# A mixture-of-experts encoder layer on one core: the row gather gets a bound, and empty slots point beyond the table

## The chip, the core and the metric

The kernel runs on one core of a Trainium2 chip. The metric is device time in microseconds (us) for one execution. The time before is the median of 3 runs, 2170.36 us (2167.73 to 2170.91). A profiled execution of the same kernel took 2169.55 us, of which 2167.7 us lie between its first and last instruction (the span).

## The reference: what is computed

One layer over 512 tokens of width 2048, in float32. Four token mixers and an output product come first. What matters here is the second half, a mixture of experts: every token picks one of 4 groups and then 2 of that group's 8 experts, so 1024 assignments fall on 32 experts, and every expert is a gated MLP (2048 to 768 to 2048).

```python
lg = h32 @ w_group + b_group
grp = jnp.argmax(lg, axis=-1)
le = take_along_axis((h32 @ w_router + b_router).reshape(t, 4, 8), grp[:, None, None], axis=1)[:, 0]
top_p, top_i = lax.top_k(softmax(le), 2)
gate = p_grp * top_p / sum(top_p)
expert = grp[:, None] * 8 + top_i
...
a = silu(xblk @ w_gate[e]) * (xblk @ w_up[e])
y = a @ w_down[e]          # each row times its gate, summed per token
```

With the inputs of setup_inputs, the reference's routing gives the experts 0 to 31 these numbers of rows: 25 18, 17 12, 15 27, 26 30, 47 36, 21 52, 33 25, 34 30, 40 20, 47 32, 38 45, 34 44, 31 25, 27 32, 44 61, 26 30 (a comma after each pair of experts). Their sum is 1024, and the largest is 61.

## The kernel before, in words

The first 676 us hold the mixers, the output product, the second norm and the router logits. The normed rows are written to a table in HBM, `h2_dram` (512 rows of 8 KB), by SyncE (line 347). VectorE then works out for every assignment a slot number: expert times 64 plus the assignment's rank within the expert (lines 1122 to 1187). An expert has 64 slots; had one more than 64 rows, a second loop (lines 453 to 457 on GpSimd) would take what is over.

The experts are worked in 16 pairs. Pair i has 128 slots: rows 0 to 63 of a tile are the even expert's, rows 64 to 127 the odd one's, each filled from rank 0 upward. The plan of a pair is a product on TensorE (`plan`, line 827): a 0/1 matrix of slot against assignment (`pick`) times the two columns of `asg`, token number and gate. A slot that nobody has gets a sum of zero in both. VectorE reads the plan (`read_plan`): `planned` gets token numbers and gates, and `gidx` the token numbers as integers (line 1209). `make_back` compares `planned` with the row `tokens`, which puts each result row back to its token. The combine adds gate times row, so that an empty slot adds zero.

GpSimd gathers the pair's rows (`gather`, line 445): 128 rows of 8 KB from `h2_dram` into `hg` (which lies in region_h), one row for each partition, by `gidx`. The first gather waits for the first plan. Every later one waits until TensorE has transposed the rows of the pair before (`hte_ps`), and is needed one pair later.

TensorE transposes 64 rows at a time (`transpose_rows`, line 837), then takes for each expert four tiles of gate and up weights (line 859) and two of down weights (line 878), and between them combines the pair before (line 850). SyncE loads the 192 weight tiles of 3 MB each into a ring of 5 buffers (lines 331 and 333). Tiles 0 to 4 are issued before the experts start; tile n waits until TensorE has used tile n - 5 (`tile_used`). The ring's buffers and the gather's rows come through the same 16 DMA engines.

The names in the rows: region_rest, region_w and region_h are parts of SBUF that hold the ring; region_h also holds `hg`; banks is PSUM; h_rows is `h2_dram`.

Of the kernel before, what the change touches and what calls it, by code (L numbers as in the profile page):

```python
# [26 lines left out]
ALU = mybir.AluOpType  # L27
# [3 lines left out]
P = 128  # L31
T = 512
# [4 lines left out]
NT = T // P  # L37
# [16 lines left out]
OVER = 2 * T // SLOTS  # L54
NA = 2 * NT
BIG = 1e30
UK = 4
NU = KT // UK
UNITS = NCH * NU
# [13 lines left out]
def build(nc, x, mix_norm, w_in, w_fourier, w_spatial, b_spatial, conv_w, w_pool, pool_scale, out_norm,  # L73
# [3 lines left out]
    with ctx:  # L77
        def sem(name):
            return ctx.enter_context(nc.semaphore(name))
# [10 lines left out]
        ps = ctx.enter_context(nc.psum_tensor("banks", [P, 8, 512], F32))  # L90
        h2_dram = nc.dram_tensor("h2_rows", (T, D), F32).ap()

        def at(off, *dims):
            n = int(np.prod(dims))
            r = min(off // R, 4)
            off -= r * R
            v = regions[r][:, off:off + n]
            if len(dims) == 2:
                v = v.rearrange("p (a b) -> p a b", a=dims[0])
            if len(dims) == 3:  # L100
                v = v.rearrange("p (a b c) -> p a b c", a=dims[0], b=dims[1])
            if len(dims) == 4:
                v = v.rearrange("p (a b c d) -> p a b c d", a=dims[0], b=dims[1], c=dims[2])
            return v
# [7 lines left out]
        h_lo = split_w1[:, 0:KT * T].rearrange("p (a b) -> p a b", a=KT)  # L112
        w_raw = [at(W0 + s * 8 * KB, UK, DG) for s in range(NU)]
        w_hi, w_lo = ([split_x[:, o:o + UK * DG].rearrange("p (a b) -> p a b", a=UK) for o in (c, c + 16 * KB)]
                      for c in (0, 8 * KB))
# [37 lines left out]
        tokens = at(o, T)  # L153
# [12 lines left out]
        asg = at(o, NT, 2, 2); o += NA * 2  # L166
        slot = at(o, NT, 2); o += NA
        gidx = [at(o + k, 1).bitcast(U32) for k in (0, 1)]; o += 2
# [12 lines left out]
        hg = at(H + 24 * KB, D)  # L181
# [80 lines left out]
        xo_ps, x2_stored = sem("xo_ps"), sem("x2_stored")  # L262
# [6 lines left out]
        counted, over_ready = sem("counted"), sem("over_ready")  # L269
        pick_ready, plan_ps, plan_read = sem("pick_ready"), sem("plan_ps"), sem("plan_read")  # L270
        slots_shifted = sem("slots_shifted")
        rows_gathered = sem("rows_gathered")
        hte_ps, hte_ready = sem("hte_ps"), sem("hte_ready")
        silu_ready, act_ready = sem("silu_ready"), sem("act_ready")
        at_ps, at_ready = sem("at_ps"), sem("at_ready")
        tokens_ready = sem("tokens_ready")
# [8 lines left out]
        OUT_TILES = NT * 4  # L285
# [6 lines left out]
        def _(sp):  # L292
# [3 lines left out]
            def w_in_unit(chunk, q):  # L296
                sp.dma_start(w_raw[q], win_v[:, q * UK:(q + 1) * UK, chunk]).then_inc(w_landed[q], 16)

# [80 lines left out]
        @block.gpsimd  # L379
        def _(pool):  # L380
            n = 0

            def made(ins):
                nonlocal n
                n += 1
                ins.then_inc(consts, 1)
                pool.wait_ge(consts, n)

            g = nc.gpsimd
            made(g.memset(ident, 0.0))  # L390
            made(g.affine_select(out=ident, in_=ident, compare_op=ALU.not_equal, fill=1.0, base=0,
                                 pattern=[[-1, P]], channel_multiplier=1))
            made(g.memset(mean_w, 1.0 / DG))
            made(g.memset(eps, EPS))
            made(g.memset(ones, 1.0))

            made(g.affine_select(out=before, in_=ones, compare_op=ALU.is_gt, fill=0.0, base=0,
                                 pattern=[[1, P]], channel_multiplier=-1))
            made(g.iota(iota, [[1, P]], 0, 0, allow_small_or_imprecise_dtypes=True))
            made(g.iota(pri4, [[-1, G]], G, 0, allow_small_or_imprecise_dtypes=True))  # L400
            made(g.iota(pri8, [[-1, EG]], EG, 0, allow_small_or_imprecise_dtypes=True))
            made(g.iota(e64, [[SLOTS, E]], 0, 0, allow_small_or_imprecise_dtypes=True))
            made(g.iota(thr, [[SLOTS, NSPLIT]], SLOTS, 0, allow_small_or_imprecise_dtypes=True))
            made(g.iota(nums, [[1, OVER]], 0, 0, allow_small_or_imprecise_dtypes=True))
            made(g.iota(asg[:, :, :, 0], [[P, NT], [0, 2]], 0, 1, allow_small_or_imprecise_dtypes=True))

            for t in range(NT):
                for q in (1, 3):
                    pool.wait_ge(ht_hi, 4 * t + q + 1)
                    full, hi, lo = (h[:, 4 * q:4 * q + 4, t * P:(t + 1) * P] for h in (h_full, h_hi, h_lo))  # L410
                    g.tensor_tensor(lo, full, hi.bitcast(F32), ALU.subtract)\
                        .then_inc(ht_lo_pool, 1)


            def split_low(u, s, q):

                pool.wait_ge(w_hi_ready, u + 1)
                pool.sem_inc(turns, 1)
                g.tensor_tensor(w_lo[s], w_raw[q], w_hi[s].bitcast(F32), ALU.subtract).then_inc(w_ready, 1)  # L419

            pool.wait_ge(x_sq, NT)
            pool.wait_ge(ht_ps, 4 * NT)
            pool.wait_ge(w_ready, 1)
            split_low(1, 1, 1)
            split_low(2, 0, 2)
            split_low(3, 1, 3)
            with pool.Fori(1, NCH) as i:
                for q in range(NU):
                    split_low(i * NU + q, q % 2, q)

            for n in range(3):
                pool.wait_ge(sq_ready, 4 * n + 4)
                for m in range(1, NH):
                    g.tensor_tensor(sq[:, 0, :], sq[:, 0, :], sq[:, m, :], ALU.add).then_inc(sq_summed, 1)
                    pool.wait_ge(sq_summed, 3 * n + m)

            pool.wait_ge(logits_ps, NT)
            g.iota(tokens, [[1, T]], 0, 0, allow_small_or_imprecise_dtypes=True).then_inc(tokens_ready, 1)

            def gather(i, first=False):  # L440
                pool.wait_ge(plan_read, i * 5 + 5)
                if not first:
                    pool.wait_ge(hte_ps, i * 2)
                pool.sem_inc(turns, 1)
                g.indirect_dma_start(out=hg, out_offset=None, in_=h2_dram,  # L445
                                     in_offset=bass.IndirectOffsetOnAxis(ap=gidx[0], axis=0))\
                    .then_inc(rows_gathered, 16)

            for b in (0, 1):
                pool.wait_ge(h2_saved[b], 32)  # L450
            for i in range(PAIRS):
                gather(i, first=(i == 0))
            n_over = pool.value_load(over_i[0:1, OVER:OVER + 1], min_val=0, max_val=OVER)
            with pool.If(n_over > 0):
                with pool.Fori(PAIRS, PAIRS + OVER_PAIRS) as i:
                    gather(i)
                pool.wait_ge(rows_gathered, 16 * (PAIRS + OVER_PAIRS))
            pool.wait_ge(rows_gathered, 16 * PAIRS)
# [3 lines left out]
        def _(ae):  # L462
# [17 lines left out]
            def gains(landed, q):  # L480
                ae.wait_ge(w_landed[q], landed)
                for k in range(UK):
                    c = C_MIX + UK * q + k
                    a.activation(w_raw[q][:, k, :], w_raw[q][:, k, :], ACT.Copy, scale=cols[:, c:c + 1])\  # L484
# [453 lines left out]
        def _(ve):  # L938
            v = nc.vector
            done = 0  # L940

            def then(ins):

                nonlocal done
                done += 1
                ins.then_inc(dve_done, 1)
                ve.wait_ge(dve_done, done)
# [191 lines left out]
            for k in (0, 1):  # L1139
# [6 lines left out]
                if k == 0:  # L1146
                    then(v.scalar_tensor_tensor(les2, oh[:, 0], -BIG, les, ALU.mult, ALU.add))
                    cur = les2
# [53 lines left out]
            def read_plan(i, s):  # L1202
                ve.wait_ge(plan_ps, i + 1)
                low, high = slice(0, SLOTS), slice(SLOTS, 2 * SLOTS)
                v.tensor_copy(planned[low, s, 0::2], ps[low, 5, 0:2]).then_inc(plan_read, 1)
                v.tensor_copy(planned[high, s, 0::3], ps[high, 5, 0:2]).then_inc(plan_read, 1)
                v.tensor_copy(planned[low, s, 1::2], ps[high, 5, 0:2]).then_inc(plan_read, 1)
                v.tensor_copy(planned[high, s, 1:3], ps[low, 5, 0:2]).then_inc(plan_read, 1)
                v.tensor_copy(gidx[0], ps[:, 5, 0:1]).then_inc(plan_read, 1)

            def make_back(i, s):
                ve.wait_ge(tokens_ready, 1)
# [28 lines left out]

            compare()
            read_plan(0, 0)
            next_compare(1)

# [88 lines left out]
```

## Time and profile before

| what | value |
|---|---|
| median of 3 runs | 2170.36 us |
| profiled execution | 2169.55 us |
| its span | 2167.7 us |
| TensorE busy | 1942.9 us (90%) |
| VectorE busy | 499.8 us (23%) |
| ScalarE busy | 257.0 us (12%) |
| GpSimd busy | 165.6 us (8%) |
| moved by DMA | 691.19 MB |
| of that on the gather's queue, q0 | 16.78 MB in 2304 packets |

Busy time is the time in which an engine had an instruction under way. The share of the DMA is the mean over its 16 engines. "Landing" is the time from the issue of a transfer until its last byte is there. Waits are put down to the instruction or the transfer that came last.

### The profile page before, as it was taken

Reading aid. Unit: us, or ns where it says so; the run is one execution under the profiler, and the core shown is the slowest. Engines: PE = TensorE matmul, PEld = TensorE weight load, DVE = VectorE, ACT = ScalarE, POOL = GpSimd, SP = SyncE. Lnnn points to the kernel's source line nnn. Section 1 sums busy time; section 2 is a strip of 40 time slices with the busy share of each in tenths; the row PEclk is TensorE's granted clock in tenths of the full one; section 3 lists DMA queues with packets and bytes.
Section 4 is the critical chain, followed back from the end, with each engine's and each line's share of the span. In section 5 each row is a group of like instructions: output and inputs, shape, how many; then the busy total and the mean of one; then the engine's idle time right before and its main releaser. Section 6 shows DMA issues by size and latency. Waiting matters only on the chain.

```text
span 2167.7 us, 20657 instructions
## 1 busy us (share of the span) xinstructions
PE 1942.9 (90%) x9337; PEld 1018.8 (47%) x9337; DVE 499.8 (23%) x667; ACT 257.0 (12%) x369; POOL 165.6 (8%) x78
## 2 busy tenths in 40 slices
PE   6999999899995998889888898988988889988895
PEld 5887885344455443434434344343443334433342
DVE  4112115500034021122211221112212122221224
ACT  5222201300000010010000100001000010000102
POOL 4444440200000000000000000000000000000000
PEclk8999999999995899999999999999999999999998
DMA  6222213091015899999999999999999999999993
GB/s 255 97 96 87 89 39 113 0 354 72 20 58 233 343 430 429 431 428 430 429 430 429 429 429 429 430 430 429 430 429 430 430 428 431 429 429 431 428 430 160
DMA packets 63043, 691.19 MB, mean 319 GB/s; under 512 B 8769, under 2 KB 9969, under 8 KB 34034
## 3 DMA queue, kind: packets, MB, share of 16 engines
q1 hardware_dynamic: 55058, 670.64, 73.7%
q0 software_dynamic: 2304, 16.78, 1.9%
q10 hardware_dynamic: 5600, 2.54, 0.4%
q8 instruction: 69, 1.13, 0.2%
q14 instruction: 12, 0.10, 0.0%
HBM read 681.55 MB, written 8.39 MB: 318 GB/s over the span
## 4 chain that ended last, share of the span: by engine, by line
PE 49%; DMA 46%; DVE 3%; issue 1%; ACT 1%; ACTq 0%; POOL 0%; POOLq 0%; PEldq 0%; DVEq 0%
DMA region_rest<-in_w_gate 25%; PE banks L859 17%; PE banks L664 14%; PE banks L774 10%; DMA region_h<-in_w_gate 9%; DMA region_w<-in_w_gate 9%; PE banks L850 3%; DMA region_rest<-in_w_up 2%; DMA region_rest<-in_w_down 1%; PE banks L719 1%; PE banks L794 1%; PE banks L878 1%; DVE region_rest L1072 1%; PE banks L785 1%; DVE region_x L1293 0%
## 5 line engine op out<-in xcount | busy, mean ns | idle before, releaser
L859 PE MATMUL banks<-region_rest,region_w 128*64 128x384 f32 x2432 | 429.6, 508 | 70.8 <-DMA region_rest<-in_w_gate 55.9
L859 PEld LDWEIGHTS banks<-region_rest,region_w 128*64 128x64 f32 x2432 | 183.3, 142 | 309.2 <-issue 233.5
L1222 DVE TENSOR_TENSOR region_x<-banks,region_x 128x1024 f32<-128x1024 f32 x128 | 151.1, 1220 | 648.9 <-PE banks L850 648.8
L664 PE MATMUL banks<-split_h,split_x 128*128 128x512 f32 x896 | 279.8, 392 | 13.6 <-DVE split_x L995 10.3
L878 PE MATMUL banks<-region_rest,region_w 128*64 128x512 f32 x960 | 229.7, 633 | 25.9 <-DVE region_w L1240 13.0
L774 PE MATMUL banks<-region_w,region_h 128*128 128x512 f32 x512 | 220.8, 593 | 2.6 <-DVE region_h L1075 2.6
L664 PEld LDWEIGHTS banks<-split_h,split_x 128*128 128x128 f32 x896 | 169.4, 189 | 51.6 <-issue 16.4
L664 PE MATMUL banks<-split_w,split_x 128*128 128x512 f32 x448 | 175.3, 391 | 0.0
L859 PE MATMUL banks<-region_w 128*64 128x384 f32 x832 | 141.2, 493 | 19.8 <-DMA region_w<-in_w_gate 16.1
L859 PE MATMUL banks<-region_h,region_w 128*64 128x384 f32 x832 | 143.1, 498 | 15.0 <-DMA region_h<-in_w_gate 12.6
L774 PEld LDWEIGHTS banks<-region_w,region_h 128*128 128x128 f32 x512 | 97.0, 190 | 124.8 <-issue 118.9
L878 PEld LDWEIGHTS banks<-region_rest,region_w 128*64 128x64 f32 x960 | 69.7, 145 | 172.1 <-issue 132.4
L850 PE MATMUL banks<-split_w 128*128 128x512 f32 x512 | 138.2, 412 | 3.9 <-DVE split_w L1228 3.6
L419 POOL TENSOR_TENSOR split_x<-region_w,split_x 128x2048 fp32r<-128x2048 f32 x27 | 124.4, 4609 | 175.1 <-DVE split_x L955 175.1
L1228 DVE TENSOR_TENSOR split_w<-banks,split_w 64x1024 fp32r<-64x1024 f32 x64 | 78.1, 1220 | 233.8 <-ACT split_w L586 232.8
L850 PEld LDWEIGHTS banks<-split_w 128*128 128x128 f32 x512 | 92.8, 192 | 60.1 <-issue 35.9
L445 POOL DMA_INDIRECT region_h<-h_rows,region_rest x16 | 15.4, 962 | 1298.0 <-PE banks L837 1279.1
L859 PEld LDWEIGHTS banks<-region_w 128*64 128x64 f32 x832 | 60.4, 138 | 97.9 <-issue 74.5
L859 PEld LDWEIGHTS banks<-region_h,region_w 128*64 128x64 f32 x832 | 61.1, 139 | 93.8 <-issue 75.4
L484 ACT ACTIVATE region_w<-region_w,region_rest 128x512 f32<-128x512 f32 x112 | 71.6, 716 | 196.2 <-DMA region_w<-in_w_in 196.2
L591 ACT ACTIVATE region_w<-banks 128x384 f32<-128x384 f32 x32 | 15.7, 492 | 651.6 <-PE banks L859 651.6
L664 PEld LDWEIGHTS banks<-split_w,split_x 128*128 128x128 f32 x448 | 84.7, 189 | 17.6 <-issue 0.2
(185 smaller groups left out, 1032.9 us busy)
## 6 DMA issues: line engine op xcount, KB each, us to landing
region_rest<-in_w_down SPq DMA_DIRECT2D x40, 3072.0 KB, 31.0
region_rest<-in_w_gate SPq DMA_DIRECT2D x39, 3072.0 KB, 31.1
region_rest<-in_w_up SPq DMA_DIRECT2D x37, 3072.0 KB, 30.7
region_w<-in_w_up SPq DMA_DIRECT2D x14, 3072.0 KB, 31.0
region_h<-in_w_up SPq DMA_DIRECT2D x13, 3072.0 KB, 30.8
region_h<-in_w_gate SPq DMA_DIRECT2D x13, 3072.0 KB, 31.0
region_w<-in_w_gate SPq DMA_DIRECT2D x12, 3072.0 KB, 32.2
region_h<-in_w_down SPq DMA_DIRECT2D x12, 3072.0 KB, 31.1
```

The source lines that it names most:

```text
L419: g.tensor_tensor(w_lo[s], w_raw[q], w_hi[s].bitcast(F32), ALU.subtract).then_inc(w_ready, 1)
L484: a.activation(w_raw[q][:, k, :], w_raw[q][:, k, :], ACT.Copy, scale=cols[:, c:c + 1])\
L664: mm = t_.matmul(ps[:, bank + m, :], w[s][:, kk, cols_m], h[:, k, :], start=(k == 0 and w is w_hi and h is h_hi), stop=(k == KT - 1 and w ...
L719: mm = t_.matmul(ps[:, (h + 1) % 4, :], ab[:, s, h, c * HD:(c + 1) * HD], dft[:, c, s, :], start=(c == 0 and s == 0), stop=(c == 1 and s = ...
L774: mm = t_.matmul(ps[:, j % 3, :], yT[:, k, t * P:(t + 1) * P], wbuf[n % 2][:, k, :], start=(m == 0), stop=(m == KT - 1))
L785: mm = t_.transpose(ps[:, 4 + q, k * P:(k + 1) * P], h2[t % 2][:, c:c + P], ident)
L794: mm = t_.matmul(ps[:, 3, t * 64:t * 64 + G + E], h2T[:, k, :], wr[:, k, :], start=(k == 0), stop=(k == KT - 1))
L850: mm = t_.matmul(ps[:, 2 + 2 * c + n, :], back[c][:, t * P:(t + 1) * P], y[c][:, n * 512:(n + 1) * 512], start=(y is y_hi), stop=(y is y_lo))
L859: mm = t_.matmul(ps[h * SLOTS:(h + 1) * SLOTS, u, 0:HF], hTe[:, k, :], ring_gu[slot][:, kk, h * HF:(h + 1) * HF], start=(k == 0), stop=(k ...
L878: mm = t_.matmul(ps[g * SLOTS:(g + 1) * SLOTS, 6 + n, :], aT[:, kk, q * SLOTS:(q + 1) * SLOTS], ring_down[slot][:, kk, (2 * c + n) * 512:( ...
L1222: v.tensor_tensor(tile, ps[:, 2 + 2 * c:4 + 2 * c, :], tile, ALU.add).then_inc(comb_added, 1)
L1228: v.tensor_tensor(y_rows(y_lo, b, c), ps[g * SLOTS:(g + 1) * SLOTS, 6:8, :], y_rows(y_hi, b, c).bitcast(F32), ALU.subtract).then_inc(y_lo_ ...
```

## The change

Token numbers are kept with 4096 taken off, in `asg` and in `tokens`, by the start values of two iotas. The plan's sum for an occupied slot is then its token minus 4096, and for an empty slot still 0. `read_plan` adds 4096 as it writes `gidx`, so that an occupied slot has its token there and an empty one 4096. The gather is given a bound of 511 with no error beyond it: it passes over those slots, and the rows of `hg` there keep what they hold. So that this is a number from the start, GpSimd clears `hg` once, ahead of the first gather. The clearing waits for the last output product (`xo_ps`), whose operand lies in the same bytes, and the gathers behind it wait for the clearing.

```diff
+NOBODY = 4096
...
-            made(g.iota(asg[:, :, :, 0], [[P, NT], [0, 2]], 0, 1, allow_small_or_imprecise_dtypes=True))
+            made(g.iota(asg[:, :, :, 0], [[P, NT], [0, 2]], -NOBODY, 1, allow_small_or_imprecise_dtypes=True))
...
             pool.wait_ge(logits_ps, NT)
-            g.iota(tokens, [[1, T]], 0, 0, allow_small_or_imprecise_dtypes=True).then_inc(tokens_ready, 1)
+            g.iota(tokens, [[1, T]], -NOBODY, 0, allow_small_or_imprecise_dtypes=True).then_inc(tokens_ready, 1)
...
                 g.indirect_dma_start(out=hg, out_offset=None, in_=h2_dram,
-                                     in_offset=bass.IndirectOffsetOnAxis(ap=gidx[0], axis=0))\
+                                     in_offset=bass.IndirectOffsetOnAxis(ap=gidx[0], axis=0),
+                                     bounds_check=T - 1, oob_is_err=False)\
                     .then_inc(rows_gathered, 16)
 
+            pool.wait_ge(xo_ps, OUT_TILES)
+            g.memset(hg, 0.0).then_inc(rows_cleared, 1)
+            pool.wait_ge(rows_cleared, 1)
             for b in (0, 1):
                 pool.wait_ge(h2_saved[b], 32)
...
-                v.tensor_copy(gidx[0], ps[:, 5, 0:1]).then_inc(plan_read, 1)
+                v.tensor_scalar(gidx[0], ps[:, 5, 0:1], float(NOBODY), None, ALU.add).then_inc(plan_read, 1)
```

On GpSimd, ahead of the experts, the order before is: the iota of `tokens`, then the 16 gathers, then the code that looks whether a second loop is needed.

```order
L434 TENSOR_TENSOR region_w<-region_w 128x512 x9
L438 IOTA region_rest 128x512
L445 DMA region_h<-h_rows,region_rest 128x2048 x16
L453 TENSOR_LOAD region_rest
L453 ISA x2
```

At the same place of the changed kernel:

```order
L435 TENSOR_TENSOR region_w<-region_w 128x512 x9
L439 IOTA region_rest 128x512
L452 MEMSET region_h 128x2048
L446 DMA region_h<-h_rows,region_rest 128x2048 x16
L458 TENSOR_LOAD region_rest
L458 ISA x2
```

One instruction is new, the clearing of `hg` (128 partitions by 2048 elements), between the iota and the first gather. Nothing else is moved on GpSimd.

On VectorE, where the first plan is read (four copies to `planned`, then `gidx`), the order before is:

```order
L1191 TENSOR_TENSOR region_w<-region_rest 128x1024
L1205 COPY region_rest<-banks 64x2
L1206 COPY region_rest<-banks 64x2
L1207 COPY region_rest<-banks 64x2
L1208 COPY region_rest<-banks 64x2
L1209 CAST region_rest<-banks 128x1
L1198 TENSOR_SCALAR region_rest<-region_rest 128x8
```

And in the changed kernel:

```order
L1196 TENSOR_TENSOR region_w<-region_rest 128x1024
L1210 COPY region_rest<-banks 64x2
L1211 COPY region_rest<-banks 64x2
L1212 COPY region_rest<-banks 64x2
L1213 COPY region_rest<-banks 64x2
L1214 TENSOR_SCALAR region_rest<-banks 128x1
L1203 TENSOR_SCALAR region_rest<-region_rest 128x8
```

The cast of 128x1 has become an addition of 128x1 at the same place. The order is otherwise the same, here and on the other engines.

## Rows read from the trace of the kernel before

**Rows 1.** The page: DMA share in tenths and GB/s, in 40 slices

```profile
DMA  6222213091015899999999999999999999999993
GB/s 255 97 96 87 89 39 113 0 354 72 20 58 233 343 430 429 431 428 430 429 430 429 429 429 429 430 430 429 430 429 430 430 428 431 429 429 431 428 430 160
```

**Rows 2.** Four stretches: busy us (x instructions) of each engine, granted clock, DMA share, GB/s

```profile
698.00:705.00 7.00, 1.94 (x16) 1.78 (x16) 0.34 (x3) 0.28 (x1) 0.00 (x0) 0.50 0.84 300
705.00:714.00 9.00, 8.20 (x34) 3.31 (x36) 0.00 (x0) 2.03 (x2) 0.00 (x0) 0.63 0.01 2
714.14:2130.23 1416.09, 1268.03 (x6888) 573.08 (x6884) 297.35 (x381) 110.53 (x125) 14.07 (x15) 0.96 1.00 427
2130.23:2167.70 37.47, 16.89 (x56) 9.03 (x56) 22.03 (x18) 12.18 (x15) 0.00 (x0) 0.75 0.28 113
```

**Rows 3.** TensorE's waits from 714 to 2131 us: us in total, times, longest us

```profile
PE banks L859 <- DMA region_rest<-in_w_gate: 55.9, 27, 4.2
...
PE banks L859 <- DMA region_w<-in_w_gate: 16.1, 8, 2.6
PE banks L859 <- DMA region_rest<-in_w_up: 13.7, 9, 1.8
```

**Rows 4.** The page: DMA queues with packets, MB, share of 16 engines' span

```profile
q1 hardware_dynamic: 55058, 670.64, 73.7%
q0 software_dynamic: 2304, 16.78, 1.9%
```

**Rows 5.** The gathers of line 445: ns min/median/max, first and last start; then landing times

```profile
L445 POOL DMA_INDIRECT region_h<-h_rows,region_rest x16: 937/939/1319, 696.1 to 1989.7; - x16
  PE banks L837: 1279.1, 15
who waited for it (us, times):
  PE banks L837: 8.6, 1
...
DMA to landing us min/median/max: 6.5/14.4/15.8
```

**Rows 6.** The chain that ended last, around the first gather: start us, us, what

```profile
694.99 0.17 DVE region_rest L1209
...
696.14 6.52 DMA region_h<-h_rows,region_rest
...
702.75 1.95 PE banks L837 x16
...
704.72 1.03 ACT region_w L580
...
705.80 23.77 PE banks L859 x128
```

**Rows 7.** GpSimd's instructions at its start: start us, us, instruction

```profile
0.79 0.20 POOL L390 MEMSET region_rest<- 128x128 f32 x1 [0.29 <-POOLq L1324]
...
1.84 0.10 POOL L394 MEMSET region_rest<- 128x1 f32 x1
...
28.77 4.58 POOL L419 TENSOR_TENSOR split_x<-region_w,split_x 128x2048 fp32r<-128x2048 f32 x1 [3.57 <-DVE split_x L955]
```

**Rows 8.** GpSimd's instructions ahead of the first gather

```profile
676.70 0.56 POOL L438 IOTA region_rest<- 128x512 f32 x1 [264.69 <-PE banks L794]
696.14 1.32 POOL L445 DMA_INDIRECT region_h<-h_rows,region_rest  x1 [18.88 <-DVE region_rest L1209]
```

**Rows 9.** VectorE around the first plan

```profile
676.55 0.17 DVE L1125 TENSOR_REDUCE region_w<-region_w 128x4 f32<-128x16 f32 x1
...
694.99 0.16 DVE L1209 CAST region_rest<-banks 128x1 uint32<-128x1 f32 x1
695.06 0.16 DVE L1198 TENSOR_SCALAR region_rest<-region_rest 128x8 f32<-128x8 f32 x1
```

More of the change, by code:

```diff
@@ L271, in build @@
         slots_shifted = sem("slots_shifted")
-        rows_gathered = sem("rows_gathered")
+        rows_gathered, rows_cleared = sem("rows_gathered"), sem("rows_cleared")
         hte_ps, hte_ready = sem("hte_ps"), sem("hte_ready")
```

## The prediction

> **What bounds the kernel now.** I read the busy slices of the page first, to find the stage in which the changed code runs. From slice 15 on the DMA engines are busy for nine tenths or more of every slice but the last, at 428 to 431 GB/s, the weight stream of the experts [rows 1]. The table by stretch makes it sharper: from 714.14 us, when SyncE issues the first tile that had to wait for a free buffer, to 2130.23 us, when the product on the last tile starts, the DMA share is 1.00 at 427 GB/s, and TensorE is busy for 1268.03 of 1416.09 us [rows 2]. So TensorE has 148 us to spare there and the DMA engines have nothing.
>
> Next I asked what TensorE waits for in that stretch. Nine rows name weight tiles and sum to 125.5 us; the three longest are shown, in short waits of 4.2 us at most [rows 3]. That is a kernel that takes each tile soon after it has landed. The count of bytes agrees: 187 tiles of 3.146 MB and 15 gathers of 1.049 MB are 604 MB, and 604 MB at 427 GB/s is 1415 us. What leaves the 16 DMA engines in this stretch leaves the time, as long as TensorE keeps up. It has to make up at most about 20 us out of 148.
>
> **What the gathers cost now.** The gather's queue carries 16.78 MB, which is 16 times 128 rows of 8 KB, in 2304 packets; its share of the 16 engines' span is 1.9%, or 41 us [rows 4]. The price of one row: 427 GB/s over 16 engines is 26.7 GB/s for one engine, so 8192 bytes take it 0.307 us. Checked the other way, 128 rows to an engine in the whole run by 0.307 us are 39.3 us, near the 41. The latency of a gather costs nothing in the stretch: it lands 14.4 us after its issue in the median, and it is issued a pair (some 90 us) before it is needed. Only one wait on a gather is on record, 8.6 us, the first [rows 5].
>
> **The change part by part.**
>
> *Rows that are no longer moved.* The experts' counts (in the section on the reference) sum to 1024 of 2048 slots, so half of the slots are empty. Pair 0 has 43 rows, and pairs 1 to 15, whose gathers lie in the saturated stretch, have 981 of 1920; 939 rows go. If the bound makes the gather drop them, the mean DMA engine loses 939 / 16 = 58.7 rows, or 18.0 us. But a weight tile is usable only when all 16 engines have brought their part, so the time follows the engine that keeps the most gathered rows, not the mean. Slots fill from rank 0 upward, so the empty ones are always the high ranks of each half, and how rows are dealt to the engines decides. The trace of before can't show the deal, because with 128 rows each engine has 8 in any deal. The bounds are:
> - the live rows dealt evenly: 18.0 us off;
> - row number modulo 16: the engine with rank 0 keeps 73 of its 120 rows in pairs 1 to 15, 47 go, 14.4 us;
> - runs of four, an engine having ranks 4k to 4k+3 and the four ranks 32 higher of one half: the engine with ranks 0 to 3 and 32 to 35 of the even experts keeps four rows in each of the 15 pairs (60), all four more where the even expert has 36 rows or more (47, 40, 47, 38, 44: 20), and 1, 2 and 2 for the ones with 33, 34 and 34. That is 85 of 120; 35 go, 10.7 us;
> - runs of eight: the engine with ranks 0 to 7 keeps all 120, since every expert has more than eight rows, and nothing is gained.
>
> I take 10.7 us, the runs of four. It is the deal near the middle of 0 to 18.0. The page "DMA: Bandwidth & Descriptors" of the Trainium skill, section "The descriptor swizzle", gives for a plain transfer to 128 partitions just this deal: engine 0 writes partitions 0 to 3 and 32 to 35, engine 8 partitions 64 to 67 and 96 to 99. No run here has shown that a gather with dropped rows keeps to it; by that page the sum stays as it is, by an even deal it would be 7 us better.
>
> *The first gather.* It is in the open: issued at 696.14, it holds TensorE for 6.52 us, and behind it come in one chain the transposes, the copy on ScalarE, and the first expert's products, whose end frees the first ring buffer at 714.14 [rows 6]. The DMA engines are idle from 705 to 714 (share 0.01) [rows 2], so what the first gather saves starts the whole stream earlier. Pair 0 has 25 and 18 rows, and with them no engine has more than 4 rows in place of 8: 4 by 0.307 us is 1.2 us off. The bounds are 0 (the wait is latency alone) and 2.5 us (all 8 rows). I take 1.2. The skill's same page, section "Anatomy of one DMA", fits such a transfer as 2.0 us and its bytes at 436 GB/s; by that the first gather would lose 1.6 us, as an estimate, and the 2.0 us would stay.
>
> *The clearing.* Not in the trace at this size. On GpSimd a MEMSET of 128x1 takes 0.10 us and one of 128x128 0.20 us; in proportion 128x2048 is 0.10 + 16 times 0.10 = 1.7 us, and the two-operand TENSOR_TENSOR of 128x2048, 4.58 us, bounds it from above [rows 7]. It can start when the iota of 676.70 is done, at 677.3 (it follows the last router logits, which come after the last output product that the clearing waits for), and the first gather waits until 696.14 for another reason, the plan [rows 8]. So it is over by 682 at the latest, with 14 us to spare: 0 us. Behind it in GpSimd's queue is only that gather. With the cover gone it would cost 1.7 us once. It runs beside VectorE's routing chain, which is on the path; were VectorE held for all of it, that would cost 1.7 us, 4.6 at the most. I take 0, since no wait joins them.
>
> *The shifted numbers.* The two iotas only start from another value. The addition for `gidx` in place of the cast is one VectorE instruction for one: CAST 128x1 0.16 us, TENSOR_SCALAR 128x8 0.16 us [rows 9]. 0 us; were it slower, 15 of the 16 lie 90 us ahead of their use.
>
> *The bound itself.* The instruction of the gather takes GpSimd 0.94 us in the median [rows 5], and the comparison with 511 may lengthen it. Only the first would show. Below, 0; above, see the last rival. I take 0.
>
> **The sum.** 10.7 + 1.2 = 11.9 us off. The profiled execution, 2169.55 us, becomes 2157.6; from the median 2170.36, 0.8 us higher, it is 2158.5 us. Its own range, with the first gather at 0 to 2.5 us and up to 1.7 for VectorE beside the clearing, is 2157 to 2161.5.
>
> **The rivals.** What a measurement of this kernel can tell from no change is about 0.2%, or 4.3 us.
> - *The rows are spread more evenly* (modulo 16, or live rows alone dealt out). Then 14.4 to 18.0 us and 1.2 go: 2151 to 2155 us. For it: a gather walks a list and could deal out what is left. Against it: the destinations are fixed rows, as before. 0.30.
> - *The bound doesn't spare the slow engine.* Either an empty slot still costs its transfer (a row read and thrown away), or the deal is in runs of eight. Then the stream is as long as before, and at most the first gather is quicker: 2169 to 2170.4 us. For it: the trace has no gather with a bound. Against it: a row that lands nowhere need not be moved. 0.14.
> - *The check makes the gather slow to issue.* If GpSimd goes through the 128 indices one by one, at the price of a smallest instruction (0.10 us for a MEMSET of 128x1 [rows 7] up to 0.16), a gather takes 13 to 20 us more to issue. Fifteen of them have 90 us of cover, but the first stands on the path with all of it. With 11.9 us gained the two are even at 0.09 us for an index, and it is slower beyond the 0.2% from 0.13 us on. With 0.16 it ends at 2158.5 + 20.5 = 2179 us; without a gain in the stream, from 0.04 us on. For it: the first gather is on the chain [rows 6]. Against it: 128 rows are now issued in 0.94 us [rows 5], which is 0.007 us for each. 0.06.
> - *The forecast*, runs of four: 0.50.
>
> **How the numbers follow.** The predicted time is that of the likeliest, 2158.5. The range of 8 in 10 has to hold the forecast and the even deals, down to 2150.5 (18.0 + 1.2 off, and 0.7 for the spread of the runs), and reaches on the other side to 2166.5, which takes in deals that spare the slowest engine only in part. The two last rivals, 0.20, stay outside. Faster by over 0.2% is the forecast and the first rival, 0.80; within 0.2% the second, 0.14; slower the third, 0.06.
>
> **What would show it.** In the changed kernel's page the gather's queue should carry 8.4 MB in place of 16.78, and HBM reads should fall by 8.4 MB. From the first waiting tile to the last product the stretch should be 1405 us and the DMA share a hair under 1.00 (the slowest engine has 85 rows and the mean 61, 7 us of 1405, so 0.995), because the engines with few rows idle: that would be the mark of an uneven deal, where an even one leaves 1.00 and 1398 us. The first wait on a gather should be about 7.4 us in place of 8.6, and the clearing should stand near 677 us with 1.7 us. The prediction is wrong if q0 still carries 16.78 MB, if the stretch doesn't shrink although the bytes do, if TensorE's waits were not spare time after all, or if the first gather's landing grows.

## The result, and the profile after

| | before | changed |
|---|---|---|
| median of 6 runs each, one session | 2169.05 us (2166.03 to 2171.74) | 2155.95 us (2154.02 to 2157.73) |
| ratio | | 0.994 (95% interval 0.9927 to 0.9953) |
| profiled execution / its span | 2169.55 / 2167.7 us | 2157.50 / 2155.6 us |

The change makes the kernel 13.1 us faster; 10.6 (2158.5 from 2169.05) to 11.9 had been forecast. The rows of the profile that answer to those of before follow. First the queues of the page (packets, MB, share of 16 engines' span):

```profile
q1 hardware_dynamic: 55058, 670.64, 74.2%
q0 software_dynamic: 2304, 8.39, 1.0%
```

Half of the gathered bytes are gone, as the counts of the experts say, but the packets are as many as in [rows 4]: a slot that is passed over leaves a small packet behind. The page counts 1024 more packets under 512 bytes than before (9793 against 8769), one for each empty slot.

The table by stretch of the changed kernel, with the same two marks as in [rows 2]: SyncE issues the first tile that had to wait for a buffer (now at 715.40 us), and the product on the last tile starts (2118.16 us). Columns: busy us (x instructions) of TensorE, its weight loads, VectorE, ScalarE, GpSimd; granted clock; DMA share; GB/s.

```profile
715.40:2118.16 1402.76, 1260.92 (x6889) 572.26 (x6885) 296.20 (x381) 110.43 (x125) 14.84 (x15) 0.97 1.00 426
2118.16:2155.60 37.44, 16.65 (x56) 8.90 (x56) 21.78 (x18) 12.18 (x15) 0.00 (x0) 0.74 0.28 113
```

This stretch, "the stream" below, is where the time went: 1402.76 us for 1416.09, 13.3 us off. What follows it is as long as before (37.44 and 37.47). TensorE's waits in it (us, times, longest) still name weight tiles:

```profile
PE banks L864 <- DMA region_rest<-in_w_gate: 45.3, 22, 4.2
...
PE banks L883 <- DMA region_rest<-in_w_down: 19.2, 12, 1.9
```

The nine rows that name weight tiles sum to 120.4 us, 5.1 less than before, although the second one shown is longer than before (12.9). TensorE's busy time fell by another 7.1 us (1268.03 to 1260.92).

The gathers of the changed kernel, line 446:

```profile
L446 POOL DMA_INDIRECT region_h<-h_rows,region_rest x16: 985/989/1282, 699.4 to 1978.7; - x16
...
who waited for it (us, times):
  PE banks L842: 6.7, 1
...
DMA to landing us min/median/max: 4.6/13.7/15.3
```

Against [rows 5], the first gather lands 4.6 us after its issue in place of 6.5, and TensorE waits 6.7 us for it in place of 8.6. The instruction on GpSimd takes 0.99 us where it took 0.94: that is all that the bound costs in issuing. Then GpSimd ahead of the first gather:

```profile
679.80 0.56 POOL L439 IOTA region_rest<- 128x512 f32 x1 [258.72 <-PE banks L799]
680.30 1.80 POOL L452 MEMSET region_h<- 128x2048 f32 x1
699.37 1.28 POOL L446 DMA_INDIRECT region_h<-h_rows,region_rest  x1 [17.27 <-issue]
```

The clearing takes 1.80 us and is over 17 us before the gather is issued. VectorE beside it:

```profile
679.31 0.31 DVE L1127 TENSOR_TENSOR region_w<-banks,region_rest 128x144 f32<-128x144 f32 x1 [2.96 <-PE banks L799]
...
681.11 0.38 DVE L1140 TENSOR_REDUCE region_w<-region_w 128x32 f32<-128x128 f32 x1
...
698.12 0.16 DVE L1214 TENSOR_SCALAR region_rest<-banks 128x1 uint32<-128x1 f32 x1
```

From the end of the logits to the index, VectorE's chain takes 18.81 us, and the instruction that has taken the cast's place 0.16 us, the same as in [rows 9]. The whole chain starts 3.1 us later in this execution than in the one of before; that is ahead of every changed instruction on the path, and the start of the stream moved between 708 and 717 us in the profiles of this study. So the span's 12.1 us are, but for rounding, 13.3 (stream) + 1.9 (first gather) - 3.2 (start of the chain, and 0.1 more from the index to the issue).

### The profile page after: what moved, and what is told of

The parts are those of the page before. It is cut to its first block, busy times and chain, and to the rows that moved or that the text cites. A ratio compares the mean times of both kernels' runs of the same rounds, so it can differ in the third digit from the quotient of the medians.

```text
span 2155.6 us, 20674 instructions
## 1 busy us (share of the span) xinstructions
PE 1937.5 (90%) x9337; PEld 1017.3 (47%) x9337; DVE 498.5 (23%) x667; ACT 257.1 (12%) x369; POOL 168.0 (8%) x79
## 2 busy tenths in 40 slices
DMA packets 63043, 682.80 MB, mean 317 GB/s; under 512 B 9793, under 2 KB 10993, under 8 KB 35058
## 3 DMA queue, kind: packets, MB, share of 16 engines
q0 software_dynamic: 2304, 8.39, 1.0%
q8 instruction: 69, 1.13, 0.2%
HBM read 681.55 MB, written 8.39 MB: 320 GB/s over the span
## 4 chain that ended last, share of the span: by engine, by line
PE 50%; DMA 45%; DVE 3%; issue 1%; ACT 1%; ACTq 0%; POOL 0%; POOLq 0%; PEldq 0%; DVEq 0%
DMA region_rest<-in_w_gate 28%; PE banks L864 17%; PE banks L669 14%; PE banks L779 10%; DMA region_h<-in_w_gate 9%; DMA region_w<-in_w_gate 6%; PE banks L855 3%; DMA region_rest<-in_w_down 2%; PE banks L883 1%; PE banks L724 1%; PE banks L799 1%; DVE region_rest L1077 1%; PE banks L790 0%; DVE region_x L1298 0%; DVE split_h L960 0%
## 5 line engine op out<-in xcount | busy, mean ns | idle before, releaser
L591 ACT ACTIVATE split_w<-banks 64x1024 fp32r<-64x1024 f32 x64 | 65.1, 1017 | 236.6 <-PE banks L883 212.7
```

What stands on the lines that cost most here:

```text
L591: a.activation(y_rows(y_hi, b, c), ps[g * SLOTS:(g + 1) * SLOTS, 6:8, :], ACT.Copy)\
```

## The experiments

In all of them the stream is read as above, from the first tile issue behind a wait to the last product. Two executions of the changed kernel agree in it to 0.5 us (1402.76 and 1403.25), so that it tells more than the medians do.

**The costs without the saving.** The constant is 0, so that an empty slot has index 0 again; bound, clearing and addition stay.

```diff
-NOBODY = 4096
+NOBODY = 0
```

> The changed kernel with the constant 4096 set to 0: the bound, the clearing and the addition for the index all stay, but an empty slot has index 0 again, so that all 128 rows are moved. If the gain is the rows that aren't moved, this is the kernel before: stretch 1416 us within 1, first gather 6.5 us from issue to landing, 2169 us within 0.2%. If part of the gain came from elsewhere (another form of the gather with a bound, say), it is faster than before; if the clearing or the bound costs on the path, slower by up to 2 us.

Measured: ratio 1.0 (0.9991 to 1.0009), 2168.05 us for 2167.63 beside it. The stream:

```profile
716.90:2133.30 1416.40, 1261.70 (x6888) 571.00 (x6885) 296.08 (x381) 110.44 (x125) 14.83 (x15) 0.96 1.00 427
```

First gather 6.7 us. The stream is within 0.3 us of the one before (1416.09). All of the gain is rows that are not moved, and the added instructions cost nothing that can be measured.

**No row at all.** The index gets 12288 more in place of 4096 more.

```diff
-                v.tensor_scalar(gidx[0], ps[:, 5, 0:1], float(NOBODY), None, ALU.add).then_inc(plan_read, 1)
+                v.tensor_scalar(gidx[0], ps[:, 5, 0:1], float(3 * NOBODY), None, ALU.add).then_inc(plan_read, 1)
```

> 12288 in place of 4096 is added to every index, so that all 128 slots of every gather are passed over: no row is moved, hg stays zero, and the experts work on zeros. It leaves out the gathered input. If each row costs its engine 0.307 us and DMA is still the bound, 120 rows go from the stretch of before: 1416.1 - 36.8 = 1379.3 us, about 2131 us in all. If TensorE became the bound on the way, or if a passed-over slot has a cost of its own, it stays longer: at 0.1 us for a slot 1391 us.

Measured: 2128.34 us, ratio 0.982 (0.9806 to 0.9834).

```profile
709.18:2089.45 1380.27, 1259.41 (x6888) 568.74 (x6884) 296.24 (x381) 110.44 (x125) 14.84 (x15) 0.96 1.00 427
```

From the run with the costs alone, 1416.40 - 1380.27 = 36.1 us for 120 rows to an engine: 0.301 us a row (0.307 had been worked out). TensorE kept up with 36 us less, so it was no bound at 13. The first gather, with no row in it, still takes 2.4 us from issue to landing.

**No gather in the stream.** Only the first gather is issued.

```diff
-            for i in range(PAIRS):
-                gather(i, first=(i == 0))
+            gather(0, first=True)
+            pool.wait_ge(over_ready, 1)
...
-                pe.wait_ge(rows_gathered, i * 16 + 16)
+                pe.wait_ge(rows_gathered, 16)
```

> Only the first gather is issued; the 15 others are left out whole, so that every pair works on the rows of pair 0. It leaves out gathered input. Against the run in which all slots are passed over it tells what a passed-over slot costs: by its packet of 4 bytes, 9 ns, 120 slots to an engine are 1 us; if a slot costs an engine a turn of 0.05 to 0.1 us, the stretch is 6 to 12 us shorter than with all slots passed over. By the price of a row alone the stretch is 1416.1 - 36.8 = 1379.3 us or less.

Measured: 2127.1 us (0.9822, 0.9806 to 0.9839), stream 1379.06 us. That is 1.2 us below the run before, for 120 slots to an engine: a slot that is passed over costs its DMA engine 0.01 us. The difference is small beside the 0.5 us between two executions, but the slot's packet of 4 bytes lasts 0.009 us in the trace.

**The changed kernel again, and two other orders of the slots.** Which row of the tile a rank gets is set by the numbers in `iota`. Both orders keep every expert's rows in its half, and move the same rows. The first spreads consecutive ranks over rows four apart; the second puts eight consecutive ranks on the rows 4k to 4k+3 and 32 higher.

```diff
-            made(g.iota(iota, [[1, P]], 0, 0, allow_small_or_imprecise_dtypes=True))
+            made(g.iota(iota.rearrange("p (a b c) -> p a b c", a=4, b=8), [[32, 4], [1, 8], [8, 4]], 0, 0, allow_small_or_imprecise_dtypes=True))
```

```diff
-            made(g.iota(iota, [[1, P]], 0, 0, allow_small_or_imprecise_dtypes=True))
+            made(g.iota(iota.rearrange("p (a b c d) -> p a b c d", a=2, b=2, c=8), [[64, 2], [4, 2], [8, 8], [1, 4]], 0, 0, allow_small_or_imprecise_dtypes=True))
```

> The changed kernel once more, beside the others of this call, since they are to be compared with it to 0.2%. From the first tile issue that waited for a buffer to the last product it had 1402.8 us (before 1416.1), so 13.3 us off. Both theories: the same, 1402.8 within 1 us, and about 2156 us in all.

> Same rows, same bytes; only the order of the slots within each expert's 64 rows is another: ranks are laid so that consecutive ranks stand four rows apart (rank k + 8j + 32h at row 32h + 4k + j). Theory A, rows dealt to the DMA engines in runs of four and the slowest engine sets the pace: that engine now keeps 69 rows of 120 in pairs 1 to 15 in place of 85, so 16 by 0.307 = 4.9 us less than the changed kernel: stretch 1397.9 us, about 2151 us in all. Theory B, dealt by row number modulo 16: the slowest engine keeps 82 in place of 73, 2.8 us more: 1405.5. Theory C, only the mean over the engines counts: no change, 1402.8.

> Same rows, same bytes, the slots in the opposite order to the spread one: rows that would share an engine in runs of four (4k to 4k+3 and 32 higher) hold eight consecutive ranks, so that one engine gets ranks 0 to 7 of every even expert. Theory A (runs of four, slowest engine): that engine keeps all 120 rows in pairs 1 to 15, and the gain of the stretch is gone: 35 by 0.307 = 10.7 us more than the changed kernel, 1413.5 to 1416 us, about 2167 in all. Theory B (modulo 16): 82 rows in place of 73, 1405.5. Theory C (mean over the engines): 1402.8, about 2156 in all.

| kernel | median, us | ratio to before (95%) | stream, us |
|---|---|---|---|
| changed, again | 2153.85 | 0.9932 (0.992 to 0.9945) | 1403.25 |
| spread | 2147.85 | 0.9909 (0.9895 to 0.9922) | 1400.28 |
| eight ranks together | 2165.19 | 0.9989 (0.9978 to 1.0) | 1415.07 |

The stream of the last of them:

```profile
710.86:2125.93 1415.07, 1253.01 (x6889) 567.96 (x6885) 296.23 (x381) 110.53 (x125) 14.88 (x15) 0.97 0.99 422
```

It moves the same 8.39 MB as the changed kernel, and the gain is gone from the stream: the gathered bytes fell by half and the time hardly at all. That kills both the mean over the engines and the deal modulo 16, and fits the runs of four. It is also what the 0.99 shows, where before had 1.00: some engines are done early. But the spread order came out 2.4 us above what theory A gave it (1397.9), and the changed kernel itself had come out 2.6 to 3.1 us below (1416.4 - 35 x 0.30 = 1405.9, measured 1403.3 and 1402.8). Something in "the engine with the most rows" was off.

**When does the final norm's row collide with the first gather?** The kernel before, with that load held back.

```diff
             sp.wait_ge(over_ready, 1)
+            sp.wait_ge(rows_gathered, 16)
             sp.dma_start(final_row, final_norm.rearrange("(a n) -> a n", a=1).to_broadcast([P, D])).then_inc(final_landed, 16)
```

> The kernel before, with the 1 MB load of the final norm's row held back until the first gather has landed. The first gather fell from 6.52 us (issue to landing) to 4.59 us with the change, 1.9 us where 1.2 was forecast. If the part above 1.2 was the collision with that load, which is issued 2.3 us after the gather, the gather lands here in about 5.8 us in place of 6.5; if it was the rows alone, in 6.5.

Measured: the first gather lands in 6.3 us (6.5 before), one run at 2170.21 us. The load explains at most 0.2 of the 1.9 us; the rest goes with the rows. With no row the first gather lands in 2.4 us, with at most four rows to an engine in 4.1 to 4.7, with eight on the fullest engine in 5.7 to 6.7, counting all kernels here and below. Three of them part the number of rows on the fullest engine from the number of rows in all. Here are 43 rows with eight on an engine (the changed kernel has 43 with four), then 8 rows on one engine, then 8 rows on two:

```profile
DMA to landing us min/median/max: 6.0/14.4/15.6
```

```profile
DMA to landing us min/median/max: 5.7/14.1/14.6
```

```profile
DMA to landing us min/median/max: 4.7/12.9/13.6
```

So four rows fewer on the fullest engine are worth 1.5 us (6.0 to 4.5) or 1.0 us (5.7 to 4.7), near the 1.2 that had been forecast. What is left of the 1.9 us goes with fewer rows in all: with eight on the fullest engine, 43 rows land in 6.0 us and 128 in 6.3 to 6.7. In the packet records of the trace a row lasts 0.41 us (before) and 0.48 us (changed) in the first gather, and 0.31 us in the stream.

**Rows of chosen engines only.** In four kernels (and a fifth, below) every gather moves the same few rows and passes over the rest, by an offset for each row of the tile. The first, for rows 0 to 3 and 32 to 35:

```diff
-NOBODY = 4096
+NOBODY = 0
...
+        skip = at(o, 1); o += 1
...
+            then(v.memset(skip[0:128], 4096.0))
+            then(v.memset(skip[0:4], 0.0))
+            then(v.memset(skip[32:36], 0.0))
...
-                v.tensor_scalar(gidx[0], ps[:, 5, 0:1], float(NOBODY), None, ALU.add).then_inc(plan_read, 1)
+                v.tensor_tensor(gidx[0], ps[:, 5, 0:1], skip, ALU.add).then_inc(plan_read, 1)
```

The others leave other rows at 0; like the first they leave out most of the gathered input. The second to the fourth were executed once each (2139.37, 2162.26 and 2159.83 us). "Number" below is the place of a DMA engine in the deal: number k has rows 4k to 4k+3 and 32 higher for k of 0 to 7, and number 8+k the same in the upper half.

> Every gather moves rows 0 to 3 and 32 to 35 of its 128, always, and passes over the other 120 always (an offset by row in place of the constant; it leaves out most of the gathered input). Runs of four, 32 apart, and the slowest engine alone sets the pace: one engine keeps 120 rows in pairs 1 to 15, the 15 others none, and the stretch is that of before, 1416 us, with a sixteenth of the bytes. If neighbours that idle make the loaded engine quicker, it is shorter by more than the 1.3 us that the kernel with ranks 0 to 7 on one engine showed (1415.1). By the mean over the engines 1416.4 - 33.9 = 1382.5; modulo 16 (two rows to each of four engines, 30 in all): 1389.5.

> The same number of rows moved, eight of each gather, but rows 0 to 7. Runs of four: two engines with four rows each, 60 in pairs 1 to 15, so half of the rows' cost goes: 1416.4 - 60 x 0.30 = 1398.4 us. Runs of eight: one engine keeps 120, 1416. Modulo 16: eight engines with 15 each, 1385.

> Rows 28 to 31 and 60 to 63 of every gather, the rest passed over: by runs of four, 32 apart, again one engine with 120 rows, but another one. The changed kernel's stretch is 2.6 us shorter than its slowest engine's 85 rows give. If the engines have paces of their own, and the one that paces the kernel before (all have 120 rows there) isn't the one with the low ranks, then this run and the one of rows 0 to 3 and 32 to 35 differ by some us, the slower at 1416. If all are alike, both are the same within 0.5 us.

> Rows 0 to 3, 32 to 35, 64 to 67 and 96 to 99 of every gather: two engines with 120 rows each. By the slowest engine the same as with one, 1415 to 1416 us; if idle neighbours are what shortens the stretch, between the one engine's and 1416.

| rows that are moved | engines by the deal | stream, us |
|---|---|---|
| none | | 1380.27 |
| 0 to 3, 32 to 35 | number 0, 120 rows | 1405.37 |
| 0 to 7 | numbers 0 and 1, 60 each | 1387.39 |
| 28 to 31, 60 to 63 | number 7, 120 | 1405.85 |
| 0 to 3, 32 to 35, 64 to 67, 96 to 99 | numbers 0 and 8, 120 each | 1406.00 |

The stream with rows 0 to 7:

```profile
713.00:2100.39 1387.39, 1251.95 (x6889) 568.04 (x6885) 296.23 (x381) 110.43 (x125) 14.84 (x15) 0.97 1.00 425
```

Eight rows of each gather cost 25 us over none when they lie in 0 to 3 and 32 to 35, and 7 us in 0 to 7. So these two runs share an engine and rows 0 to 7 don't. But three expectations failed alike: 1405 to 1406 where 1416 was expected, and 1387 where 1398 was. The run with number 7 met its own expectation for engines that are all alike (within 0.5 us of number 0), but it too lies below 1416. All four are short by about the same 11 us (10.6, 11.0, 10.2 and 10.0 in the order of the table), however many rows they move. If idle neighbours had helped, two loaded engines should have been slower than one by more than the 0.6 us seen. A constant that doesn't depend on the rows looks like a head start: with no rows these engines need about 1369.3 us, and another one sets the 1380.3.

If so, the pace of every kernel is that of the engine that is late to begin with, as long as no other passes it, and its rows must explain all streams. Number 9 has rows 68 to 71 and 100 to 103, which are ranks 4 to 7 and 36 to 39 of the odd experts: 60 rows in pairs 1 to 15, and four more for each of 52, 45, 44 and 61, so 76 in the changed kernel. That gave the last run.

```diff
+            then(v.memset(skip[0:128], 4096.0))
+            then(v.memset(skip[64:72], 0.0))
+            then(v.memset(skip[64:68], 4096.0))
+            then(v.memset(skip[96:104], 0.0))
+            then(v.memset(skip[96:100], 4096.0))
```

> Every gather moves rows 68 to 71 and 100 to 103 alone, by the deal in runs of four the rows of the tenth engine, number 9. With no row moved the stretch is 1380.3 us; with 120 rows on number 0 it is 1405.4, on number 7 1405.9, on numbers 0 and 8 1406.0, with 60 on each of numbers 0 and 1 1387.4. Theory D, the engines don't start equal: one of them is some 11 us behind without any rows and sets the 1380.3, the others stand at about 1369.3 (1369.3 + 120 x 0.30 = 1405.3; + 60 x 0.30 = 1387.3). Number 9 is the only one whose rows fit the others: 76 in the changed kernel (1380.3 + 22.7 = 1403.0, measured 1402.8 and 1403.3), 67 in the spread order (1400.3, measured 1400.3), 116 with ranks 0 to 7 together (1414.9, measured 1415.1), 120 before (1416.1, measured 1416.1). So this run is at 1380.3 + 35.8 = 1416.1 us. Theory E, idle neighbours make a loaded engine quicker and the engines are alike: 1405.5, as number 0 and number 7.

Its stream, and under it that of the run with rows 0 to 3 and 32 to 35:

```profile
713.07:2130.22 1417.15, 1261.90 (x6888) 572.21 (x6884) 296.14 (x381) 110.42 (x125) 14.84 (x15) 0.97 0.98 416
```

```profile
710.76:2116.13 1405.37, 1257.79 (x6889) 569.72 (x6885) 296.25 (x381) 110.55 (x125) 14.88 (x15) 0.97 0.99 420
```

Eight rows in each gather in both, 1.06 MB on the gather's queue in both, and 11.8 us between them. With rows on number 9 alone the kernel is exactly as slow as before, where all 128 are moved: 2168.74 us, ratio 1.0001 (0.999 to 1.0013); with rows on number 0 alone the ratio is 0.9955 (0.9943 to 0.9967). Theory E is out. The share of 0.98 agrees: in this run the other engines wait for number 9.

The trace also holds what makes number 9 late. Besides the rows and tiles, the queue of instruction loads (q8 of the page) has 54 packets of 16 KB in the stream. The packets of one DMA engine follow each other within some ns, so that they can be strung together from their starts and durations, and the gathered rows say which string is which engine. As far as the strings can be followed without doubt, in the runs above none of 24 instruction packets in a row lies on number 0, and none of 21, 19 and 40 on number 7, number 8 and number 1. On number 9 lie the 18th and the 26th of the execution and none of the 16 others that can be followed. With no rows each such packet costs its engine 1.55 us: it lasts 1.06, and the weight packet behind it 0.49 longer than the usual 0.91. If number 9 takes every eighth, as these two say, it has 7 in the stream, 10.9 us: the 11 us by which it is late. No run moves the instruction packets, so the seven are inferred from the two; the other five last 1.06 to 1.08 us in that run, as the two do, where loads on engines that wait last as little as 0.90.

## Why the prediction was right, point by point

- **What bounds the kernel.** Right. The stream followed the DMA engines down to 1379 us, and TensorE kept up each time. The mark that the prediction named, a DMA share of 0.995, can't be told from the table's 1.00. The packets' times, summed over the stream, give 1.000 before and 0.997 changed.
- **The price of a row**, 0.307 us: right, 0.301 measured.
- **The rows.** Right: 8.39 MB. The remark that HBM reads would fall was wrong as to the page: that line reads 681.55 MB before and after, though 8.4 MB fewer were moved. It fell only when whole gathers were left out (665.83).
- **The deal.** Runs of four, the second run 32 rows up, was chosen as the middle of the bounds. No row of before spoke for it, so that part of the choice was luck. Shown: rows 0 to 3 and 32 to 35 share an engine (25 us), rows 0 to 7 are two engines' (7 us), and rows 68 to 71 and 100 to 103 share one again (37 us over none). The rule of the page "DMA: Bandwidth & Descriptors" of the Trainium skill, section "The descriptor swizzle", agrees, also for a gather that passes over rows.
- **Which engine sets the pace.** This is the mis-sized term: "the engine with ranks 0 to 3 and 32 to 35 of the even experts" keeps 85 rows, and 10.7 us were to go. Measured: 13.3. That engine isn't the pace-setter. One that is 11 us behind it without any rows is, and number 9 is shown to be such a one; with 76 rows in place of 120 it gains 44 x 0.301 = 13.2 us. The prediction took all engines as equal but for their gathered rows. Number 0 with its 85 is at 1369.3 + 85 x 0.301 = 1394.9 us, long done.

The same two numbers, 1380.3 for number 9 without rows and 0.301 a row, give every stream below; the first row is no test, since the price of a row was taken from a stream with all 120:

| kernel | rows on number 9 | worked out | measured |
|---|---|---|---|
| before | 120 | 1416.4 | 1416.1 |
| changed | 76 | 1403.2 | 1402.8, 1403.3 |
| spread | 67 | 1400.5 | 1400.3 |
| eight ranks together | 116 | 1415.2 | 1415.1 |
| only number 9's rows | 120 | 1416.4 | 1417.2 |

- **The first gather.** 1.9 us in place of 1.2, inside the bounds of 0 to 2.5: the four rows of the fullest engine are worth 1.0 to 1.5, and the prediction put nothing for having fewer rows in all. The fit of the same page, section "Anatomy of one DMA" (2.0 us and the bytes at 436 GB/s), has a floor near the 2.4 us measured without rows, but gives 4.4 us for the full gather, where 6.3 to 6.7 were measured.
- **The clearing, the addition, the bound.** 0 was right: 1.80 us under cover, 0.16 for 0.16, 0.05 us in the issue, and 0.1 from the index to the issue. VectorE's chain from the logits to the index took 18.81 us beside the clearing, 18.78 before (676.21 to 694.99), so it was not held.
- **The sum.** 11.9 us forecast, 12.1 in the profiled executions, 13.1 in the medians. That the first two agree so closely is luck: 15.2 us were saved from the first gather on, and the profiled execution of the changed kernel reached its routing chain 3.1 us later.
- **The rivals.** The even deal (2151 to 2155 us) lay close to the measured median (2155.95), but its mechanism is out: with eight ranks together the same rows gain 1.0 us in the stream. The second (a passed-over slot still costs its transfer) fell to the 0.01 us for a slot. The third (slow to issue) fell to the 0.05 us.

The spread order beats both kernels: 2147.85 us, 6.0 below the changed kernel's 2153.85 in the same session. Of these, 3.0 are in the stream, as number 9's nine rows fewer give (2.7), and 0.4 in the first gather. The rest lies ahead of the stream, where the two kernels run the same instructions, and isn't claimed.

## What to carry to other kernels

When a stage is bound by DMA, count bytes for each DMA engine and not for the core: a transfer that all engines must finish is as late as the one with the most work, and saved rows on the others were worth nothing here. Work out where the skipped rows sit in the tile, since padding need not be spread evenly (here it all sat in the high ranks), and lay live rows so that they thin out on the engine that is last. A gather with a bound was cheap here (0.01 us for each row that is passed over, against 0.30 for one that is moved), but one row to an engine is the unit that is saved.

## What the runs showed of the hardware that was not expected

- The 16 DMA engines aren't equal in this kernel. With no gathered rows, number 9 needs about 1380.3 us for its part of the stream, and numbers 0, 1, 7 and 8 about 1369.3 by the runs that load them. A DMA share of 1.00 before hides that 0.8%.
- Instruction loads (q8 of the page: 69 packets, 1.13 MB) go over some of these engines and not over others. They are small in bytes, but at 1.55 us for each packet seven of them come to the 11 us.
- Number 9 need not be the only late one. The durations of the instruction packets repeat every eight (1.02, 1.02, 1.07, 1.07, 1.06, 1.10, 1.10, 1.09 us), which points to eight engines in turn. Number 10, with 76, 67 and 108 rows in the changed, the spread and the third order, would fit the streams as well. Only numbers 0, 1, 7, 8 and 9 were loaded alone or in pairs, so which the others are stays open.
- Passed-over rows stay as small packets in the queue: 2304 packets with all rows, with half of them, and with none; the trace has them at 4 bytes.
- The page's line on HBM reads counts rows that a gather has passed over: 681.55 MB with all rows, with half and with none.
